# Two transformer layers' branch projections as products of split halves, and ScalarE's finer wait in the turning stage

## The reference, cut to what matters

```
h = rms(x, g_mix) * (1 + sc1) + sh1
parts = h @ w_in                          # q, k, v of both branches, and two gates
y_a = gqa_attention(...) @ w_branch_a     # (512 x 512) @ (512 x 1024)
y_b = dilated_attention(...) @ w_branch_b # (512 x 256) @ (256 x 1024)
mixed = sigmoid(gate_a) * y_a + sigmoid(gate_b) * y_b
x = x + gt1 * (mixed @ w_out)
... then rms, w_ff1, squared relu, w_ff2
```

## Time and profile before

| | |
|---|---|
| median of 3 runs | 2471.11 us (2467.51 to 2471.56) |
| the profiled execution | 2468.32 us, its span 2466.5 us |
| granted TensorE clock, mean | 0.977 |
| PE busy | 2330.3 us, 94% of the span |
| DVE busy | 1488.6 us, 60% |
| ACT busy | 607.1 us, 25% |
| POOL busy | 1119.5 us, 45% |

### The profile page before, as it was taken

One profiled execution on the slowest core, in us unless ns is written; L12 is line 12 of the kernel. 1 busy time (PEld: TensorE's weight loads), 2 busy tenths in 40 slices (PEclk: granted clock), 3 DMA queues, 4 the chain that ended last, 5 costly groups with the idle time before them and its releaser, 6 DMA issues.

```text
span 2466.5 us, 28621 instructions
## 1 busy us (share of the span) xinstructions
PE 2330.3 (94%) x11549; PEld 1812.9 (74%) x11549; DVE 1488.6 (60%) x1806; ACT 607.1 (25%) x1242; POOL 1119.5 (45%) x608
## 2 busy tenths in 40 slices
PE   7798879999999999999999999999999999999998
PEld 6676746786666778777567788887877767788886
DVE  6998265454343696554478866768656437855341
ACT  3133234422221311253113332311125320100000
POOL 5443241042333566422164666666642207666663
PEclk9899999999999899999999999999999999999999
DMA  6345661234444432211144556543321204222321
GB/s 190 104 114 137 203 210 60 78 116 134 137 137 137 139 103 94 90 35 35 52 154 132 175 174 194 192 154 120 103 81 35 52 18 153 86 94 94 103 96 42
DMA packets 262752, 280.72 MB, mean 114 GB/s; under 512 B 29709, under 2 KB 231633, under 8 KB 262621
## 3 DMA queue, kind: packets, MB, share of 16 engines
q1 hardware_dynamic: 238124, 243.24, 31.4%
q10 hardware_dynamic: 24496, 35.66, 4.5%
HBM read 257.87 MB, written 17.85 MB: 112 GB/s over the span
## 4 chain that ended last, share of the span: by engine, by line
PE 54%; DVE 9%; issue 2%; ACT 1%; ACTq 0%; DVEq 0%
PE ps L446 31%; PE ps L572 6%; PE ps L2199 3%; PE ps L2200 3%; PE ps L2201 3%; PE ps L888 2%; PE ps L931 2%; PE ps L907 1%; DVE ps L999 1%; DVE ada_acc L361 1%; DVE squared L2555 1%; PE ps L917 1%; DVE hidden_high L2556 1%; DVE hT_low L766 1%; DVE work L2257 1%
## 5 line engine op out<-in xcount | busy, mean ns | idle before, releaser
L233 POOL TENSOR_SCALAR ring_high<-ring 128x1024 fp32r<-128x1024 f32 x302 | 354.9, 1175 | 1289.4 <-PE ps L572 369.5
L235 POOL TENSOR_TENSOR ring_low<-ring,ring_high 128x1024 fp32r<-128x1024 f32 x302 | 767.6, 2542 | 25.2
L446 PE MATMUL ps<-hT_high,ring_high 128*128 128x512 f32 x704 | 282.3, 401 | 1.0 <-DVE hT_low L766 0.6
L446 PE MATMUL ps<-hT_high,ring_low 128*128 128x512 f32 x704 | 274.4, 390 | 0.0
L446 PE MATMUL ps<-hT_low,ring_high 128*128 128x512 f32 x704 | 274.2, 390 | 0.0
L572 PE MATMUL ps<-hT_high,ring_high 128*128 128x512 f32 x568 | 241.8, 426 | 18.5 <-POOL ring_low L235 11.2
L361 DVE TENSOR_REDUCE ada_acc<-ring 128x256 f32<-128x2048 f32 x48 | 188.3, 3923 | 106.3 <-ACT ring L348 106.3
L572 PE MATMUL ps<-hT_high,ring_low 128*128 128x512 f32 x568 | 228.8, 403 | 0.0
L572 PE MATMUL ps<-hT_low,ring_high 128*128 128x512 f32 x568 | 228.5, 402 | 0.0
L348 ACT ACTIVATE ring<-ring,c_act 128x256 f32<-128x256 f32 x384 | 158.5, 497 | 231.0 <-DMA ring<-in_w_ada_dram 222.6
L446 PE MATMUL ps<-hidden_high,ring_high 128*128 128x512 f32 x512 | 201.1, 393 | 0.0
(11 more groups left out here) (386 smaller groups left out, 4128.7 us busy)
## 6 DMA issues: line engine op xcount, KB each, us to landing
ring<-in_w_in_dram SPq DMA_DIRECT2D x75, 1024.0 KB, 5.3
ring<-in_w_ff_dram SPq DMA_DIRECT2D x64, 1024.0 KB, 5.3
ring<-in_w_ada_dram SPq DMA_DIRECT2D x48, 1024.0 KB, 7.1
ring<-in_w_out_dram SPq DMA_DIRECT2D x12, 1024.0 KB, 6.2
scratch_x<-xT ACTq DMA_DIRECT2D x3, 2048.0 KB, 8.6
xT<-scratch_x ACTq DMA_DIRECT2D x3, 2048.0 KB, 8.6
ring<-in_w_mem_kv_dram SPq DMA_DIRECT2D x4, 1024.0 KB, 5.6
ring<-in_w_branch_a_dram SPq DMA_DIRECT2D x8, 512.0 KB, 6.1
```

Of the source, the lines that this page charges most:

```text
L233: nc.gpsimd.tensor_scalar(hi, raw, 1.0, 1.0, ALU.mult, ALU.mult).then_inc(hi_done.sem, 1)
L235: nc.gpsimd.tensor_tensor(lo, raw, hi.bitcast(F32), ALU.subtract).then_inc(lo_done.sem, 1)
L446: return nc.tensor.matmul(out[0:rows, bank, cols[0]:cols[1]], lhsT, rhs, start=start, stop=stop)
```

## The change

1. The slabs `m{l}pa0`, `pb`, `pa1` (not split) become four slabs `m{l}{mp}p` that are split, each 256 columns of w_branch_a over the same columns of w_branch_b (6 blocks of rows; three DMAs each).
2. `ya` and `yb` get a high and a low part. POOL splits the four blocks of `ya` during attention b (`split_ya`, placed in its list between the last gate half and the first branch half); ScalarE rounds the two blocks of `yb` and VectorE makes their low parts between attention b and the mixing. The high parts lie where attention b's keys and third probabilities buffer were, so POOL waits for score step 4 and, for the last block, for the transposes of step 6.
3. A mixing tile is 18 matmuls on split parts in place of 6 plain ones. PE waits for `ya_split` before the first, for `yb_split` before the thirteenth.
4. The rounding of `mixed` goes from VectorE to ScalarE (`mix_high`), and VectorE makes the low part of tile m-1 inside tile m (`mixed_low`). The out stage counts `mixed_split` where it counted `tile_taken`.
5. In the turning ScalarE waits for `qkv_done` less two, not for the last.

```diff
-        add(f"m{l}pa0", T["w_branch_a_2"][l], (0, 512), 0, D, False, part=0, pairs=True, width=512)
-        add(f"m{l}pb", T["w_branch_b_2"][l], (0, 256), 0, D, False, width=D)
-        add(f"m{l}pa1", T["w_branch_a_2"][l], (0, 512), 0, D, False, part=1, pairs=True, width=512)
+        for mp in range(4):
+            add(f"m{l}{mp}p", T["w_branch_a_2"][l], (0, 512), 0, D, part=mp, pairs=True, below=(T["w_branch_b_2"][l], 256))
...
+                    if waits is not None and (n, j) in waits:
+                        pe.wait_ge(*waits[(n, j)])
...
-    with K.stage(tensor_entry={}) as block:
+    entry = {**K.last, "vector": (DO.sem, DO.total - 2)}
+    with K.stage(entry, tensor_entry={}) as block:
...
         @block.vector
         def _(e):
+            e.wait_ge(DO.sem, DO.total)
...
+    def split_ya(pool):
+        pool.wait_ge(copied.sem, copied0)
+        pool.wait_ge(scored.sem, scored0 + 4)
+        for k in range(4):
+            if k == 3:
+                pool.wait_ge(transposed.sem, transposed0 + 18)
+            nc.gpsimd.tensor_scalar(highs[k], rows_of[k], 1.0, 1.0, ALU.mult, ALU.mult).then_inc(ah.sem, 1)
+            pool.wait_ge(ah.sem, ah0 + k + 1)
+            nc.gpsimd.tensor_tensor(lows[k], rows_of[k], highs[k].bitcast(F32), ALU.subtract).then_inc(al.sem, 1)
+
+    K.turn_before(K.half_of[K.first[f"m{l}0p"]], split_ya)
...
+        @block.scalar
+        def _(e):
+            high_part(4)
+            e.wait_ge(copied.sem, copied.total)
+            high_part(5)
+
+        @block.vector
+        def _(e):
+            for k in (4, 5):
+                low_part(e, k)
...
-        K.link(e, "dve_step", v.tensor_tensor(x, x, y, ALU.add))
-        K.link(e, "dve_step", v.tensor_copy(split[0][:, m, :], x))
-        return v.tensor_tensor(split[1][:, m, :], x, split[0][:, m, :].bitcast(F32), ALU.subtract)
+        if m >= 1:
+            mixed_low(e, m - 1)
+        return v.tensor_tensor(x, x, y, ALU.add)
+
+    def mix_high(e, m):
+        e.wait_ge(xs_made.sem, gated + m + 1)
+        nc.scalar.activation(split[0][:, m, :], mixed[:, m % 2, 0, :], ACT.Copy).then_inc(xh.sem, 1)
...
-    tiles_stage(K, tiles, 2, dve=mix_dve)
+        pairs = [p for k in range(6) for p in ((hi[:, k, :], highs[k]), (hi[:, k, :], lows[k]), (lo[:, k, :], highs[k]))]
+        tiles.append(products(0, P, (0, SEQ), pairs[:12], (slab, m % 2)) + products(1, P, (0, SEQ), pairs[12:], (slab, m % 2)))
+    tiles_stage(K, tiles, 2, dve=mix_dve, also=mix_high, waits={(0, 0): (al.sem, al0 + 4), (0, 12): (yl.sem, yl0 + 2)})
```

More of the change, by code:

```diff
@@ L242, in plan_slabs, with add @@
     K.first = {}
-    def add(name, w, rows, col0, cols, split=True, part=None, pairs=False, width=SLAB_W):
+    def add(name, w, rows, col0, cols, split=True, part=None, pairs=False, width=SLAB_W, below=None):
         nonlocal halves
@@ L265, in add @@
                     K.deep.add(len(K.slabs))
-            K.slabs.append((ap, (rows[1] - rows[0]) // P, n, split))
+            K.slabs.append((ap, deep, n, split))
     K.ada_after = {}
@@ L2470, in layer @@
                     [252 + 13 * i for i in range(10)] + [384, 384])
+    with K.stage({}) as block:
+        @block.scalar
[7 more added lines that the diff above has]
+                low_part(e, k)
+    ah.total += 4
+    al.total += 4
+    yh.total += 2
+    yl.total += 2
     K.close(stream=stream.taken)
@@ L2487, in layer @@
-        tiles.append(products(0, P, (0, SEQ), [(wa[:, k, :], ya[:, k, :]) for k in range(4)], (sa, None))
-                     + products(1, P, (0, SEQ), [(wb[:, k, :], yb[:, k, :]) for k in range(2)], (sb, None)))
-    before, xb, mt = dict(K.last), K.sig("x_back"), K.sig("tile_taken")
-    gated = mt.total
-    tiles_stage(K, tiles, 2, dve=mix_dve)
-    with K.stage(before) as block:
-        @block.scalar
+        slab = K.first[f"m{l}{m // 2}p"]
+        hi, lo = K.half(slab, m % 2)
+        pairs = [p for k in range(6) for p in ((hi[:, k, :], highs[k]), (hi[:, k, :], lows[k]), (lo[:, k, :], highs[k]))]
@@ L2495, in _ @@
+        tiles.append(products(0, P, (0, SEQ), pairs[:12], (slab, m % 2)) + products(1, P, (0, SEQ), pairs[12:], (slab, m % 2)))
+    before = dict(K.last)
+    tiles_stage(K, tiles, 2, dve=mix_dve, also=mix_high, waits={(0, 0): (al.sem, al0 + 4), (0, 12): (yl.sem, yl0 + 2)})
+    with K.stage({}) as block:
+        @block.vector
         def _(e):
-            e.wait_ge(mt.sem, gated + 4)
-            e.dma_start(K.xT[:, :, :], sx).then_inc(xb.sem, 16)
+            mixed_low(e, KD - 1)
+    xh.total += KD
@@ L2511, in out_dve @@
         return add_square(K, e, K.xT[:, n, :], n, square[:, 0, :])
-    tiles_stage(K, column_tiles(K, K.first[f"out{l}"], KD, KD, split), 1, dve=out_dve, arriving=(mt, gated, before, 5))
+    tiles_stage(K, column_tiles(K, K.first[f"out{l}"], KD, KD, split), 1, dve=out_dve, arriving=(xl, xl0, before, 5))
     with K.stage() as block:
```

38 lines of the change are left out of this document (33 added, 5 removed).

## The result

| | before | after |
|---|---|---|
| median | 2470.64 us, 4 runs (2467.51 to 2471.56) | 2447.65 us, 4 runs (2445.54 to 2451.78) |
| profiled execution, span | 2466.5 us | 2450.0 us |
| granted TensorE clock, mean of that execution | 0.977 | 0.975 |

The ratio after/before is 0.9911, with a 95% interval of 0.9893 to 0.9929: about 22 us less (17.5 to 26.4; the medians alone are 23.0 us apart). The forecast was 2448.5 us, range 2442 to 2457. The profiled execution of after took 2451.78 us, the slowest of its four.

A forecast was written before the change was run, and what follows sets the result against it. PE, busy 94% of the span, was taken to bound the kernel. Terms of -17.0 (mixing), -6.8 (turning), +1.0 (attention b) and +1.0 (door) gave -21.8 us; from 2471.1 that is 2449.3, stated as 2448.5 us, range 2442 to 2457.

The forecast's parts named there:

- The mixing on PE: Mixing stage: split products in place of plain ones take PE from 41.2 to 32.7 us, gaining 8.5 us a layer.
- The rival of slow products: Mixing: split products do not run at 0.2274 us; at 0.28 us nothing is gained there, leaving 2465 us; chance 0.03.
- The door: Start of the mixing: VectorE's low parts of yb may come late beside POOL's split, costing 0.5 us a layer, bounds 0 and 1.2.
- The turning: Turning stage: ScalarE's earlier table load and copies remove PE's wait for aq, gaining 3.4 us a layer, 6.8 in all.
- the rival that the wait only moves: Turning: VectorE's copies or last step hold PE at a later turn, so the 6.8 us stay (2455 us); chance 0.08.
- POOL in attention b: Attention b: POOL's new splits delay VectorE where two delays meet in a step, costing 0.5 us a layer, bounds 0 and 2.
- VectorE's lag: Mixing into out stage: last mixed_low at 42.5 us against 42.3 needed, just hidden; cost 0, bounds 0 and 3.3.
- The rival in which it comes through: Longest delays beside POOL for every half: PE waits up to 3.3 us a layer for mixed_split (2449 to 2456); chance 0.16.
- The out stage: Out stage: PE's waits for POOL merge into one and are not lost; taken as 0, bound a gain of 2.9 us.

The follow-up runs named there:

- the run with the turning alone: The kernel before with only ScalarE's earlier entry into the turning added: 2464.55 us, ratio 0.9965 against before.
- the two others: The changed kernel run again without edits, on two chips: 2448.67 us (ratio 0.9906 against before) and 2450.44 us (ratio 0.9908).
- The slab order: The changed kernel with the first layer's two w_ada slabs placed after the second and third w_out slabs, not first and second: 2444.92 us, ratio 0.9885 against before.
- the kernel with the projections alone: The changed kernel with ScalarE's old entry into the turning, so without part 5 of the change: 2463.20 us, ratio 0.9955 against before.

## Why the prediction was right, step by step

Taken by stages, the trace of after gives -21.7 us, and the sum was -21.8. The total is closer than the terms: mixing and door -15.6 (-16.0 in the sum), turning -9.9 (-6.8), attention b +2.6 (+1.0), out stage +0.9 (0), attention a +0.3 (0). That the sum came out to 0.1 us is luck: a turning that gave 3.1 us more hides 3.2 us that the four other terms gave less. What was right is the mechanism of the mixing, the door and the turning.

- **The mixing on PE** (predicted 41.2 to 32.7 a layer). Right: 33.1 us with the door's loss in it, products 0.227 us apart, at a clock of 1.00. The 41.2 was 0.3 too much: from first product to first product before is 40.9. Gain with the door 15.6 us in two layers, where the sum had 16.0. The rival of slow products is refuted by this spacing.
- **The door** (0.5 a layer). Mechanism right, size near: POOL holds up VectorE's low parts, 2.81 us for two, and PE loses 0.23 us there. Its wait for the gate is 0.99 us, 0.1 more than before.
- **The turning** (3.4 a layer). ScalarE's early load, the five copies ahead of PE's need and VectorE's copies in time all came as written; the rival that the wait only moves is refuted by the run with the turning alone. The size was wrong in the second layer, 6.3 us, and the two layers' 9.9 us lie outside my own bounds of 0 and 6.8. I had priced the wait from its own row and not looked at the granted clock behind it.
- **POOL in attention b** (0.5 a layer, bounds 0 and 2). First layer 0.5 longer. The second layer's 2.1 is for 1.5 us not POOL's: the kernel with the turning alone, with no new work on POOL, has it too (77.5 against 76.0), and the clock's fall behind an unchanged wait of PE explains it. What is left is about 0.5, nearly all of it by a meeting of two instructions (0.84 us of wait where 0.41 is usual) and not in proportion to the work.
- **VectorE's lag** (0, last low part at 42.5 against 42.3 needed). The lag is smaller than I made it: 40.3 us after the mixing's start (1239.66 - 1199.33), needed at 42.7. The estimate of 16 us of delay beside POOL was somewhat high, and the 42.5 is 0.4 more than its own terms (4.1 and 38) add up to. The rival in which it comes through did not happen, but it was 2.3 us away: with the rounding back on VectorE its last low part came 3.5 us later, and PE waited 1.0 us for it.
- **The out stage** (0, with a gain of 2.9 as the bound). This step failed, in its sign for the profiled execution. The two waits did merge into one, as I wrote, of 3.08 us where they were 1.16 and 1.71. I took "merged and not lost" for no cost. But the single wait is followed by six microseconds at the lower clock, which the two short ones were not. The stage became 1.3 us longer in that trace, and 0.6 shorter in the two others, with a shorter wait. The slab order shows that this wait and its clock held 4 to 6 us.

The two largest misses, 3.1 us more gain in the turning and 1.6 us less in attention b, and the out stage's sign as well, are one omission: what the clock does behind a wait of PE. In the turning and the out stage a wait was priced at its length; in attention b a wait that the change leaves alone was followed by the lower clock after the change and not before.

## What to carry to other kernels

Where true float32 products bound a stage and other engines idle there, three products of split halves cut PE's time by a fifth (0.858 to 0.682 us); count first what VectorE gets beside POOL's splits, for it came within 2.3 us of holding PE up. When a wait on TensorE is to be priced, read the granted clock of the microseconds behind it too, add half of the time at the lower level to the wait's length, and look twice at an edit that merges two short waits into a long one. An engine's wait on entering a stage should name the last step that it needs, at the cost of a line: here that was 8.7 us (5.7 to 11.6).

## What the runs showed of the hardware that was not expected

- A PE wait of some 3 us may cost far more than its length. Read from two kernels with and without it, the wait of 3.37 us cost 6.3 us (second layer's turning), the one of 3.08 us 6.0 and the one of 2.46 us 4.2 (out stage). Behind them PE worked at a granted clock of 0.50 for 5.9, 5.9 and 3.2 us, and the wait plus half of that time gives 6.3, 6.0 and 4.1. In before the clock had fallen about a microsecond before PE began again (a mean of 0.86 from 1822.50 to 1826.00). It is not certain: the wait of 3.38 us in the first layer's turning cost 3.6, the 3.37 us of the second layer in the kernel with the projections alone 4.8, and attention b of before, with the same wait of 2.78 us in both layers, took 77.5 us in the one and 76.0 in the other. Behind the waits of 1.16, 1.71 and 1.20 us the clock stayed at 1.00. What decides between these cases was not found out. The Trainium skill (TensorE: Matmul & The Clock Gate, HAM oscillation) tells of pauses between groups of products after which the next group starts at the lower clock. The traces agree for these waits, though not for each one, and show it for a single pause in a stage that is busy otherwise.
- Beside POOL's TENSOR_SCALAR a VectorE TENSOR_SCALAR on 128x2 elements took 0.61 us, where it took 0.17 in the step before. The earlier trace rows showed such a delay for TENSOR_TENSORs of 512 columns only, and I had counted on no other kind. But the trace of before had it already, in the first layer's attention b. Timelines of POOL and VectorE in before:

```profile
1133.63 1.05 POOL L233 TENSOR_SCALAR ring_high<-ring 128x1024 fp32r<-128x1024 f32 x1 [11.15 <-PE ps L572]
1133.66 1.03 DVE L1003 TENSOR_SCALAR negmax<-rowmax 128x2 f32<-128x2 f32 x1
```
